# Small first transfers, four slabs in the first four k tiles, and spreading products in the rounded format

## The reference

```python
h = _rmsnorm(x, e_norm_pre)            # x * rsqrt(mean(x*x) + eps) * gain
p = h @ w_in                           # 2048 -> 7 * 1024
a_x, a_b, a_c, a_z, b_val, b_gate, b_z = jnp.split(p, 7, axis=-1)
ya = a_b * _causal_dwconv(a_c * a_x, a_conv)
yb = _causal_dwconv(b_val * jax.nn.sigmoid(b_gate), b_conv) + b_conv_bias
yb = jax.nn.silu(_layernorm(yb, b_ln_g, b_ln_b))
u = jnp.concatenate([ya * jax.nn.silu(a_z), yb * jax.nn.silu(b_z)], axis=-1)
return u @ w_out
```

## Time and profile before

| | us |
|---|---|
| median of three runs | 1307.91 |
| lowest and highest | 1307.6, 1308.23 |
| the profiled execution's own time | 1307.34 |
| its span | 1305.5 |
| TensorE busy | 1295.1 (99%) |
| VectorE busy | 1018.6 (78%) |
| ScalarE busy | 528.8 (41%) |
| POOL busy | 142.4 (11%) |

### The profile page before, as it was taken

The page is one execution under the profiler, slowest core; times in us unless marked ns, Lnnn a source line. Parts: engine busy times, 40 slices in busy tenths (PEclk is TensorE's granted clock), DMA queues, the critical chain, the costliest instruction groups (busy, mean ns, idle before and its releaser), DMA issues.

```text
span 1305.5 us, 17052 instructions
## 1 busy us (share of the span) xinstructions
PE 1295.1 (99%) x7006; PEld 1128.1 (86%) x7006; DVE 1018.6 (78%) x979; ACT 528.8 (41%) x595; POOL 142.4 (11%) x129
## 2 busy tenths in 40 slices
PE   9999999999999999999999999999999999999997
PEld 7888888888888888888888889999999999888886
DVE  6489999999955645444985899957888888899788
ACT  6521213213131212223555667654444445455452
POOL 0000000000006700000000110101213332000000
PEclk9999999999999999999999999999999999999999
DMA  9736677666567888862685576864344435674157
GB/s 325 228 92 199 162 229 232 193 185 190 166 188 217 257 266 279 243 198 87 236 312 193 178 208 210 281 189 121 114 122 125 136 112 169 251 242 144 54 204 258
DMA packets 260085, 254.39 MB, mean 195 GB/s; under 512 B 5488, under 2 KB 212464, under 8 KB 255024
## 3 DMA queue, kind: packets, MB, share of 16 engines
q1 hardware_dynamic: 253984, 243.03, 59.3%
q10 hardware_dynamic: 4512, 5.42, 1.3%
q0 software_dynamic: 1520, 4.98, 1.0%
HBM read 214.87 MB, written 38.54 MB: 194 GB/s over the span
## 4 chain that ended last, share of the span: by engine, by line
PE 99%; DMA 0%; DVE 0%; ACT 0%; DVEq 0%; issue 0%; SPq 0%; ACTq 0%
PE bank L1031 33%; PE bank L1033 33%; PE bank L1035 33%; PE bank L1067 1%; DMA raw<-e_in 0%; DVE rows L2541 0%; PE bank L1118 0%; PE bank L1105 0%; PE bank L1131 0%; PE bank L1125 0%; DVE w_lo L1887 0%; DVEq L151 0%; ACT w_hi L1387 0%; DVE rows L2173 0%; ACT junk L1518 0%
## 5 line engine op out<-in xcount | busy, mean ns | idle before, releaser
L1031 PE MATMUL bank<-h_hi,w_hi 128*128 128x512 f32 (+1 forms) x1472 | 520.2, 353 | 0.3 <-DVE w_lo L1887 0.3
L1033 PE MATMUL bank<-h_lo,w_hi 128*128 128x512 f32 (+1 forms) x1472 | 518.5, 352 | 0.0
L1035 PE MATMUL bank<-h_hi,w_lo 128*128 128x512 f32 (+1 forms) x1472 | 518.4, 352 | 0.0
L1031 PEld LDWEIGHTS bank<-h_hi,w_hi 128*128 128x128 f32 x1472 | 278.6, 189 | 38.7 <-issue 1.3
L1033 PEld LDWEIGHTS bank<-h_lo,w_hi 128*128 128x128 f32 x1472 | 278.7, 189 | 37.8 <-issue 0.7
L1035 PEld LDWEIGHTS bank<-h_hi,w_lo 128*128 128x128 f32 x1472 | 278.6, 189 | 37.5
L1845 DVE TENSOR_TENSOR w_lo<-raw,w_hi 128x2048 fp32r<-128x2048 f32 x60 | 148.4, 2473 | 33.7 <-ACT w_hi L1360 32.8
L1031 PE MATMUL bank<-w_hi,h_hi 128*128 128x512 f32 x448 | 174.5, 389 | 0.0
L1035 PE MATMUL bank<-w_hi,h_lo 128*128 128x512 f32 x448 | 174.3, 389 | 0.0
L1033 PE MATMUL bank<-w_lo,h_hi 128*128 128x512 f32 x448 | 174.3, 389 | 0.0
L1360 ACT ACTIVATE w_hi<-raw 128x2048 fp32r<-128x2048 f32 x60 | 113.9, 1908 | 93.6 <-PE bank L1035 66.4
(11 more groups left out here) (175 smaller groups left out, 1479.7 us busy)
## 6 DMA issues: line engine op xcount, KB each, us to landing
raw<-e_in SPq DMA_DIRECT2D x52, 1024.0 KB, 5.9
scratch<-e_out SPq DMA_DIRECT2D x17, 1024.0 KB, 7.4
scratch<-o_in SPq DMA_DIRECT2D x24, 512.0 KB, 7.6
pair_sums<-scratch SPq DMA_DIRECT2D x24, 512.0 KB, 6.5
spare<-e_out SPq DMA_DIRECT2D x12, 1024.0 KB, 7.6
rows<-o_in SPq DMA_DIRECT2D x24, 512.0 KB, 4.2
spare<-o_out SPq DMA_DIRECT2D x12, 1024.0 KB, 6.5
raw<-o_in SPq DMA_DIRECT2D x22, 512.0 KB, 4.2
```

The lines of the kernel that those rows point to most:

```text
L1031: nc.tensor.matmul(dst, w[0], m[0], start=first, stop=False, skip_group_check=goes_on)
L1033: nc.tensor.matmul(dst, w[0], m[1], start=False, stop=False, skip_group_check=goes_on)
L1035: return nc.tensor.matmul(dst, w[1], m[0], start=False, stop=last, skip_group_check=goes_on)
```

## The change

- The first transfers get smaller. After x tile 0 one transfer brings k tile 0 of slabs 0 and 1 (into row 2 of `scratch`), then come x tile 1, k tiles 1 to 3 of slabs 0 and 1 (into `raw`), then quarter 0 of slabs 2 and 3 (two transfers into rows 0 and 1 of `scratch`), then x tiles 2 and 3 and the rest as before. SP issues 26 transfers instead of 25 up to the last weight quarter. x tiles 8 to 15 share semaphores in pairs.
- `vecs` comes in two: the 16 `pre` columns first, the other 328 columns from ScalarE's queue after it has rounded the four first quarters.
- TensorE runs k tiles 0 and 1 of slabs 0 and 1, k tiles 0 and 1 of slabs 2 and 3, k tiles 2 and 3 of all four, then k tiles 4 to 15 of slabs 0 and 1, then 4 to 15 of slab 2, then of slab 3. ScalarE and VectorE split in that order. The warm-up stays at eight products.
- POOL clears `csum` and `vsum` only after the two first low parts, since row 2 holds the first tile.
- The three spreading products: `ones`, the diagonals and the column sums are in the rounded format, in a high and a low part, and each product becomes two (`summed`). VectorE makes four low diagonals after the four high ones, twice; for `csum` ScalarE makes the high part (in row 0) and VectorE the low part (in row 1), in step 8 behind the work of slab 1.

```diff
+FIRST_TILE, FIRST_REST = (0, 1), (1, QUARTER)
+FIRST_PIECES = [*((q, *FIRST_TILE) for q in range(2)), *((q, *FIRST_REST) for q in range(2)),
+                *((q, *FIRST_QUARTERS[0]) for q in range(2, 4)),
+                *((q, *FIRST_QUARTERS[j]) for j in range(1, 4) for q in range(2)),
+                *((q, *FIRST_QUARTERS[j]) for q in range(2, 4) for j in range(1, 4))]
...
-        diagonals = sb("diagonals", [P, TT, P])
+        diagonals = sb("diagonals", [P, TT, P], F32R)
...
+        diagonal_lows = sb("diagonal_lows", [P, TT, P], F32R, at=scratch_at + 5 * T * 4)
...
-        ones = sb("ones", [P, P])
+        ones = sb("ones", [P, P], F32R)
...
             load_x(slice(0, 1), x_first_loaded)
+            load_first_tiles()
+            load_x(slice(1, 2), x_loaded[0])
+            for n in range(RAW):
+                load_first(n, 0, *FIRST_REST)
+            load_first_quarters()
+            load_x_pair(1)
+            for j in range(1, 4):
+                load_x_pair(2 * j)
                 for n in range(RAW):
...
+                    load_first(n, j, *FIRST_QUARTERS[j])
                 load_x_pair(2 * j + 1)
...
+            pool.wait_ge(first_lo, 2)
             nc.gpsimd.memset(csum, 0.0).then_inc(consts_set, 1)
...
             keep_warm(8)
...
-            for k in range(KT):
+            for k in range(2):
                 pe.wait_ge(x_lo_ready, k + 1)
                 for q in range(RAW):
                     first_product(q, k)
+            for k in range(2):
+                for q in range(RAW, SLOTS):
+                    first_product(q, k)
+            for k in range(2, KT):
+                pe.wait_ge(x_lo_ready, k + 1)
+                for q in range(SLOTS if k < QUARTER else RAW):
+                    first_product(q, k)
             for q in range(RAW, SLOTS):
-                for k in range(KT):
+                for k in range(QUARTER, KT):
                     first_product(q, k)
 
+            def summed(dst, hi, lo):
+
+                nc.tensor.matmul(dst[:, :], ones[:, :], hi, start=True, stop=False)
+                return nc.tensor.matmul(dst[:, :], ones[:, :], lo, start=False, stop=True)
...
-                    pe.wait_ge(diagonals_ready, TT)
-                    nc.tensor.matmul(bank[R_BANK][:, :], ones[:, :], diagonals[:, :, :],
-                                     start=True, stop=True).then_inc(x_spread, 1)
+                    pe.wait_ge(diagonals_ready, 2 * TT)
+                    summed(bank[R_BANK], diagonals[:, :, :], diagonal_lows[:, :, :])\
+                        .then_inc(x_spread, 1)
...
-            pe.wait_ge(csum_ready, CB)
+            pe.wait_ge(csum_ready, CB + 2)
...
-            act.dma_start(vecs[:, :], vec).then_inc(vec_loaded, 16)
+            pre = AT_VEC["pre"]
+            act.dma_start(vecs[:, pre:], vec[:, pre:]).then_inc(pre_loaded, 16)
...
+            act.wait_ge(pre_loaded, 16)
+            act.wait_ge(x_first_loaded, 16)
+            x_rounded(0)
+            act.wait_ge(first_tile_loaded, 16)
+            for q in range(RAW):
+                first_split(q, *FIRST_TILE)
+            act.wait_ge(x_loaded[0], 16)
+            x_rounded(1)
+            for q in range(RAW):
+                act.wait_ge(first_loaded[q][0], 16)
+                first_split(q, *FIRST_REST)
+            act.wait_ge(first_quarter_loaded, 32)
+            for q in range(RAW, SLOTS):
+                first_split(q, *FIRST_QUARTERS[0])
+            act.dma_start(vecs[:, 0:pre], vec[:, 0:pre]).then_inc(vec_loaded, 16)
...
+                    if (i, q) == (0, 1):
+                        act.wait_ge(csum_ready, CB)
+                        nc.scalar.activation(csum_hi[:, :], csum, ACT.Copy).then_inc(csum_ready, 1)
...
+                dve.wait_ge(diagonals_ready, before + TT)
+                for t in range(TT):
+                    nc.vector.scalar_tensor_tensor(
+                        out=diagonal_lows[:, t, :], in0=ident[:, :], scalar=token_power[:, t:t + 1],
+                        in1=f32(dst[:, t, :]), op0=ALU.mult, op1=ALU.subtract)\
                         .then_inc(diagonals_ready, 1)
```

More of the change, by code:

```diff
@@ L260, in build @@
         x_first_loaded = sem("x_first_loaded")
-        x_loaded = [sem(f"x_loaded{p}") for p in range(KT // 2)]
+        x_loaded = [sem(f"x_loaded{n}") for n in range(6)]
         x_tok_loaded = [sem(f"x_tok_loaded{n}") for n in range(2)]
@@ L362, in build, with first_raw, x_load, first_lows @@
         gain_next_loaded = sem("gain_next_loaded")
+        def first_raw(q, start, end):
+            if (start, end) == FIRST_TILE:
+                return first_tile[:, 1 - q, :]
+            if q >= RAW and start == 0:
+                return first_quarter[:, SLOTS - 1 - q, :]
+            return raw[:, q % RAW, start * P:end * P]
+        def x_load(pair):
+            return pair if pair < 4 else pair // 2 + 2
+        def first_lows(q, start, end):
+            n = FIRST_PIECES.index((q, start, end))
+            return sum(1 for piece in FIRST_PIECES[:n + 1] if piece[2] < KT)
         def f32(ap):
@@ L526, in load_x_pair, with load_first, column_pair, load_first_tiles @@
             def load_x_pair(pair):
[L528 to L535, removed]
+                load_x(slice(2 * pair, 2 * pair + 2), x_loaded[x_load(pair)])
+            def load_first(q, j, start, end):
+                sp.dma_start(first_raw(q, start, end).rearrange("p (k c) -> p k c", c=P),
+                             columns(e_in, E1A_ORDER[q])[:, start:end, :])\
+                    .then_inc(first_loaded[q % RAW][j], 16)
+            def column_pair(first, apart):
+                return e_in.rearrange("(k p) n -> p k n", p=P)[:, :, first:first + apart + P]\
+                    .rearrange("p k (n c) -> p n k c", c=P)[:, ::apart // P]
+            def load_first_tiles():
+                pair = column_pair(B_VAL, B_GATE - B_VAL)
+                sp.dma_start(first_tile, pair[:, :, 0, :]).then_inc(first_tile_loaded, 16)
+            def load_first_quarters():
+                pair = column_pair(A_X, A_C - A_X)
+                for n in range(2):
+                    sp.dma_start(first_quarter[:, n, :].rearrange("p (k c) -> p k c", c=P),
+                                 pair[:, n, 0:QUARTER, :]).then_inc(first_quarter_loaded, 16)
             def load_tokens(t):
@@ L1074, in keep_warm @@
                 for _ in range(count):
-                    nc.tensor.matmul(bank[0][:, 0:P], ones[:, :], ident[:, :],
+                    nc.tensor.matmul(bank[0][:, 0:P], f32(ones[:, :]), ident[:, :],
                                      start=True, stop=True)
             def first_product(q, k):
[L1080 to L1084, removed]
+                for piece in FIRST_PIECES:
+                    if piece[0] == q and piece[1] == k and piece[2] < KT:
+                        pe.wait_ge(first_lo, first_lows(*piece))
+                    elif piece[0] == q and piece[1] == k:
+                        pe.wait_ge(lo_ready, q + 1)
                 last = product(bank[4 + q][:, :], weights(q, k, P), operand(k),
@@ L1115, in _ @@
                 feature_major(i, operand)
[L1116 removed]
+            pe.wait_ge(csum_ready, CB + 2)
             pe.wait_ge(bank_free[4], uses4(4, "stat") + 1)
[L1118 to L1119 removed]
+            summed(bank[4], csum_hi[:, :], csum_lo[:, :]).then_inc(stat_ready, 1)
             with pe.Fori(E1A + 1, E1A + E1B - 1) as i:
```

118 lines of the change are left out of this document (65 added, 53 removed).

## The result

The changed kernel takes 1311.42 us in the median of nine runs (1310.09 to 1313.24), the kernel before beside it 1307.67 (1307.46 to 1308.23): a ratio of 1.0026, 95% interval 1.0017 to 1.0034. The changed kernel is 3.7 us slower by the medians. The forecast was 1306.5 (1305.3 to 1307.8), 1.4 us faster than the three runs known then, so the time lies outside the range and on the other side.

What follows compares the result with a forecast made beforehand. TensorE, busy 99% of the span, was taken as the bound. Spreading products 1.22 plus start 0.2 made 1.4 us: profiled 1307.34 to 1305.9, timed median 1307.91 to 1306.5, range 1305.3 to 1307.8.

Steps and rivals of the forecast that it cites:

- theory B: From the experiments, not the prediction: the early quarters' half MB and longer work in front delay token rows and diagonals.
- waits give part back: Rival at the first spreading product and early quarters: TensorE waits 0.7 us at 56, 0.3 earlier; 1307.5 us, chance 0.17.
- the starved ramp: Rival near 12 us: early quarters land late, TensorE stands 4.2 us, kernel 2.8 us slower, 1310.7; chance 0.06.
- the rounded pairs at the float32 pace: Rival at the three spreading products: each pair takes 2 x 0.86 us, giving 1310.3 us; chance 0.02.
- The spreading products: Three places in TensorE's chain: each falls from 0.86 to 0.453 us, saving 0.41 each, 1.22 us in all.
- The start: TensorE's first product: 0.3 to 0.5 us earlier, held by the warm-up, at the lower clock worth 0.2 us.
- The mean granted clock of 0.998: Sign for a slow start: about 2.6 us lost, some 5 us at half clock from the warm-up's start.
- Four slabs in the first four k tiles: TensorE's reordered first products: costs nothing, since operands for slabs 2 and 3 fit by 0.1 to 0.5 us.
- the landing of the early quarters: DMA of quarter 0 of slabs 2 and 3: 1.57 MB landed at about 7.6 to 7.9 us.
- The 64-byte vector columns: The `pre` columns ahead of ScalarE's start, about 3.7: held up past 4.1 the 0.2 gain shrinks, past 4.5 gone.

Runs made afterwards that it cites:

- shared: The kernel before with x tile pairs 4 and 5, and 6 and 7, sharing semaphores, nothing else: 1310.69 us, ratio 1.0021.
- own: The changed kernel with a semaphore for each pair of x tiles again, no instruction added or moved: 1307.98 us, ratio to before 0.9997.
- spreads: The kernel before with only the three spreading products changed to rounded high and low parts: 1307.23 us, ratio 0.9993.
- own_late: The changed kernel with a semaphore for each x tile pair and the first spreading product twelve products later: 1307.39 us, ratio 0.9993.
- own_f32: The changed kernel with a semaphore for each x tile pair and float32 spreading products: 1308.68 us, ratio to before 1.0000.
- after_late: The changed kernel, semaphores still shared, with the first spreading product twelve products later: 1307.83 us, ratio to before 0.9997.
- spreads_late: The kernel before with rounded spreading products, the first of them twelve products later: 1307.42 us, ratio 0.9994.
- after_f32: The changed kernel with the three spreading products in float32 as before: 1310.18 us, ratio to before 1.0025.

## Why the prediction was wrong

- **The step that failed.** The prediction asked of each later x tile only when TensorE wants it, found it wanted later than before, and concluded that nothing later is thin. It put at most 1.5 us of delay on the last weight quarters, against 0.8 us of cover on the first spreading product, and even that only in a rival. It left at nothing, without a reason, a part of the change that it had in front of it: that x tiles 8 to 15 share semaphores in pairs. TensorE indeed waited for no x tile; ScalarE did, and its split of the weights, SP's next loads and the diagonals stood behind it. That wait can't be seen in any row of before, and counting bytes doesn't show it, since it lies in which landing a wait names. ScalarE's split of the last quarter came at 25.76 instead of 19.68; the semaphores alone made 3.7 us in shared (23.36), and without them own still had 3.6 (23.26), 2.5 less than the changed kernel. So the two overlap, and theory B's part was 3.6 us at this split, not 1.5; how much of it is the queue and how much the order wasn't taken apart. Further down, SP issued the token rows at 29.38 instead of 24.09 (27.19 in own, 28.43 in shared), and the high diagonals began at 57.32 instead of 53.35 (55.59 and 57.72). The semaphores explain the loss in time, since own without them took 1307.98; the new start alone is 2.2 of the 4.0 us by which the diagonals were late.
- **The rival that came true** was the first one, that waits give part back: right in its place (the first spreading product, behind the DMA-fed diagonals) and in its chain, but priced at 0.7 us where 2.55 were measured, and without the clock's fall behind it, 1.6 us and more. Even this rival (chance 0.17) had the kernel 0.4 us faster; only the starved ramp and the rounded pairs at the float32 pace had it slower, both by another path.
- **The spreading products** were right: 0.39 to 0.41 us saved at each of three in spreads, 0.41 at the second and third in the changed kernel. The second and third found their parts ready.
- **The start** was right in its first number only. TensorE began at 5.88, 0.74 earlier; I had 0.3 to 0.5, as the warm-up's records run on over the first product for longer than the 0.16 us that I allowed (2.51 + 3.62 is 6.13, 0.25 after the product's start; 0.35 in own). In that execution the products ran at full pace almost at once, so the clock had risen by 5.9; in own, own_late and own_f32 they took 0.43 us up to about 8, in shared up to 10.5. The moment differs from run to run, as the Trainium skill says in "TensorE: Matmul & The Clock Gate", Part 1; the traces agree, and one trace was too little to price it. The mean granted clock of 0.998, which I took as a second sign of the slow start, is none. The windows of the kernel before give 1.00 for the first 8 us, where the pace was the lower one, and 0.50 only from 1301 us to the end, where TensorE has finished; 4.5 us at half are 2.25 us, enough for that mean. So at the start the level is read from the pace and not from this column.

```profile
3.00:4.00 1.00, 1.00 (x7) 1.00 (x7) 0.00 (x0) 0.00 (x0) 1.00 (x18) 1.00 0.95 273
...
1301.00:1302.00 1.00, 0.00 (x0) 0.00 (x0) 1.00 (x3) 0.00 (x0) 0.00 (x0) 0.50 0.70 230
```

- **Four slabs in the first four k tiles** was called the thinnest cover, 0.1 to 0.5 us. It wasn't enough: 0.36 and 0.98 us were waited. The step that failed is the landing of the early quarters, 9.08 for 7.6 to 7.9. I had taken the rates of before, 302 to 359 GB/s; the small transfers on one queue brought 222 and 195 at 3 to 5 us.
- **The 64-byte vector columns** landed 3.0 us after their issue, as the whole vectors had in 3.1. ScalarE's first tile still waited for them and began at 3.82, for 4.00 before and 3.7 in the forecast: no loss and little gain. No run took their effect apart. The Trainium skill's rule on transfers under 512 bytes ("DMA: Bandwidth & Descriptors", Specifications) doesn't show in the latency of this one.

## What to carry to other kernels

Where two transfers share a semaphore and the kernel waits for both counts, the first is as late as the second: before sharing one, look at what lies between them on the queue and who is behind the waiting engine. When a change moves the start of a DMA-fed chain, follow the chain to the next place where the bound engine needs its result, and price the miss with the fall of the clock, not only with the wait. If the cover is thin, moving the consumer by a few products may be the cheapest repair: it brought 3.6 us in after_late and cost nothing that can be measured in spreads_late.

## What the runs showed of the hardware

- After TensorE stood 2.4 us its granted clock was at 0.50, 1.2 GHz, for some 3.4 us, in the changed kernel's trace; after 1.7 us in the traced execution of after_f32 it was not.
- The rise of the clock at the start, read from the pace, lay between 5.9 us (the changed kernel) and about 10.5 (shared, where 512 columns still took 0.43 us at 10.06) with the same warm-up, which moved the arrival at the first spreading product by more than the forecast gain of the start.
- One queue with transfers of 128 to 256 KB, each 0.40 to 0.51 us in the issue, moved 195 GB/s at 4 to 5 us (131 to 217 in the other traces with this start); with two of them on a second queue it was 310 to 323. With the old start, whose transfers are 256 KB and more, one queue moved 343 to 346.
